# 128 bytes of unused SBUF ahead of the low parts of the input

## The reference, cut to what matters

```python
def _trunk(x, ...):
    for layer in range(DEPTH):                      # DEPTH = 2
        if layer % 2 == 0:
            m = _ab_mixer(x, ...)                   # x @ w_in_ab, attention and retention heads, @ w_out_ab
        else:
            m = _ssd_mixer(x, ...)                  # x @ w_in_ssd, convolution, scan, gate, @ w_out_ssd
        x = _layer_norm(DN_ALPHA * x + m, ...)
        f = _conv_ffn(x, ...)                       # (silu(g) * u) @ w_down, with g, u = conv(x @ w_up)
        x = _layer_norm(DN_ALPHA * x + f, ...)
```

## Time and profile before

| | |
|---|---|
| median of 3 runs | 3045.04 us (3043.46 to 3046.95) |
| the profiled execution, span | 3044.3 us |
| PE busy | 3001.3 us (99%) |
| PEld busy (beside PE) | 2936.1 us (96%) |
| DVE busy | 1977.1 us (65%) |
| ACT busy | 1623.5 us (53%) |
| matmuls of L664 to L666 | 3 x 7552 = 22,656 |
| mean granted TensorE clock | 0.995 |

### The profile page before, as it was taken

One profiled execution on the slowest core, in us unless ns is written; L12 is line 12 of the kernel. 1 busy time (PEld: TensorE's weight loads), 2 busy tenths in 40 slices (PEclk: granted clock), 3 DMA queues, 4 the chain that ended last, 5 costly groups with the idle time before them and its releaser, 6 DMA issues.

```text
span 3044.3 us, 60261 instructions
## 1 busy us (share of the span) xinstructions
PE 3001.3 (99%) x25064; PEld 2936.1 (96%) x25064; DVE 1977.1 (65%) x2508; ACT 1623.5 (53%) x1735; POOL 175.6 (6%) x317
## 2 busy tenths in 40 slices
PE   9999999999999999999999999999999999999997
PEld 9999899999999999999999999999999999999997
DVE  5454454677665566767767888876776665566665
ACT  4435575545444444545556767775564444445453
POOL 1010101000000000000002222210000000000000
PEclk9999999999999999999999999999999999999998
DMA  7565667544444545544467788874444444555452
GB/s 271 185 236 208 222 221 276 197 160 165 176 168 182 200 167 206 186 182 162 159 224 258 273 295 277 298 263 188 184 158 185 188 165 179 193 194 177 181 191 83
DMA packets 100667, 614.99 MB, mean 202 GB/s; under 512 B 12912, under 2 KB 13184, under 8 KB 39456
## 3 DMA queue, kind: packets, MB, share of 16 engines
q1 hardware_dynamic: 68688, 498.17, 43.8%
q0 software_dynamic: 31824, 114.61, 11.3%
HBM read 575.44 MB, written 37.28 MB: 201 GB/s over the span
## 4 chain that ended last, share of the span: by engine, by line
PE 90%; DVE 5%; ACT 2%; issue 1%; DMA 1%; POOL 0%; DVEq 0%; POOLq 0%; SPq 0%; ACTq 0%
PE acc L664 29%; PE acc L665 28%; PE acc L666 28%; DVE lo L574 1%; PE aux L2130 1%; DMA extra<-xds 1%; DVE x L1816 1%; DVE xl L1829 1%; DVE x L1824 1%; PE aux L2479 0%; ACT hi L564 0%; PE aux L2460 0%; ACT xh L1223 0%; PE aux L2215 0%; PE aux L2228 0%
## 5 line engine op out<-in xcount | busy, mean ns | idle before, releaser
L664 PE MATMUL acc<-xh,hi 128*128 128x264 f32 x7552 | 2177.3, 288 | 9.2 <-DVE lo L574 4.2
L665 PE MATMUL acc<-xl,hi 128*128 128x264 f32 x7552 | 2147.3, 284 | 0.0
L666 PE MATMUL acc<-xh,lo 128*128 128x264 f32 x7552 | 2139.6, 283 | 0.0
L664 PEld LDWEIGHTS acc<-xh,hi 128*128 128x128 f32 x7552 | 1423.6, 189 | 31.1 <-issue 19.5
L665 PEld LDWEIGHTS acc<-xl,hi 128*128 128x128 f32 x7552 | 1423.6, 189 | 1.8
L666 PEld LDWEIGHTS acc<-xh,lo 128*128 128x128 f32 x7552 | 1420.5, 188 | 0.0
L574 DVE TENSOR_TENSOR lo<-raw,hi 128x2048 fp32r<-128x2048 f32 x473 | 1077.5, 2287 | 378.8 <-ACT hi L564 378.0
L564 ACT ACTIVATE hi<-raw 128x2048 fp32r<-128x2048 f32 x473 | 897.7, 1907 | 490.0 <-DMA raw<-in_w 322.4
L563 ACT ACTIVATE xh<-pj 128x1056 fp32r<-128x1056 f32 x144 | 156.0, 1084 | 338.2 <-PE acc L666 279.8
L571 DVE TENSOR_TENSOR xl<-pj,xh 128x1056 fp32r<-128x1056 f32 x144 | 180.7, 1255 | 201.8 <-ACT hi L564 199.3
L1539 DVE SCALAR_TENSOR_TENSOR stage<-acc,par,stage 128x255 f32<-128x255 f32 x352 | 168.7, 479 | 23.1 <-DVE stage L1539 21.9
(11 more groups left out here) (287 smaller groups left out, 1617.3 us busy)
## 6 DMA issues: line engine op xcount, KB each, us to landing
raw<-in_w SPq DMA_DIRECT2D x473, 1024.0 KB, 4.9
x<-in_ssm POOLq DMA_DIRECT2D x32, 512.0 KB, 7.4
out_ssms<-x POOLq DMA_DIRECT2D x32, 512.0 KB, 7.2
x<-in_ret POOLq DMA_DIRECT2D x16, 512.0 KB, 5.6
out_rets<-x POOLq DMA_DIRECT2D x16, 512.0 KB, 4.3
x<-in_ck POOLq DMA_DIRECT2D x16, 512.0 KB, 4.4
x<-in_cv POOLq DMA_DIRECT2D x16, 512.0 KB, 5.8
pj<-cumd POOLq DMA_DIRECT2D x32, 256.0 KB, 7.2
```

Of the source, the lines that this page charges most:

```text
L664: pe.matmul(out, hi[:, s, w], xh[:, a, :], start=kc == 0 and k == 0, stop=False)
L665: pe.matmul(out, hi[:, s, w], xl[:, a, :], start=False, stop=False)
L666: m = pe.matmul(out, lo[:, r, w], xh[:, a, :], start=False, stop=kc == ph.kc - 1 and k == CK - 1)
```

## The change

One line is added: a buffer of 32 floats (128 bytes of each partition) between `xh` and `xl`, which nothing reads or writes. `raw`, `lo`, `x` and `xh` keep their places; `xl`, `pj`, `hi` and everything behind begin 128 bytes later. No instruction, semaphore or transfer is added, removed or put in another order.

```diff
         x_ = sb("x", [P, KT * T])
         xh = sb("xh", [P, KT, T], F32R)
+        sb("row_half", [P, 32])
         xl = sb("xl", [P, KT, T], F32R)
         pj = sb("pj", [P, AB_TILES * T])
```

## The result

The changed kernel takes 3057.22 us (median), against 3046.84 us for the kernel before beside it. The ratio is 1.0039, with a 95% interval of 1.0029 to 1.0049: slower by some 12 us (the medians are 10.4 us apart), where no change was forecast. The profiled execution has a span of 3057.7 us against 3044.3, 13.4 us more.

The account below looks back on a forecast made before the run. PE's step from product to product was taken to bound the kernel. Swapped chunk times added 0.4 us, all else 0: 3044.7 us on the span, 3045.4 us as median; likeliest 3045 us, 8-in-10 range 3029 to 3064 us.

Parts of the forecast that it names:

- What bounds the kernel: Whole kernel: PE, busy 99% of the span, sets the time by its step between products (L664 to L666); no producer does.
- That 128 bytes count, and as a distance modulo 256: Products in up0: even chunks take 5.80 us, odd ones 5.85, because input tiles start 128 bytes apart modulo 256.
- Which operands meet: L664 to L666: passing tile meets weights loaded for the next product: `xh` with `hi`, `xl` with `lo`, `xh` with next `hi`.
- term 1: Products: all three tile-weight pairs shift by 128 bytes, so even and odd chunks swap 5.80 and 5.85 us; +0.4 us.
- The bounds from the nearest steps: Products: every step of twelve like the fastest, 1.44 us, or the slowest, 1.47 us; 3014 to 3071 us.
- rival A: Loads of `hi` in L664 and L665: the weights' own place costs 16 us, giving 3061 us; 0.22 together with the mirror of B.
- the mirror of B: Products: the passing tile's own place puts all even chunks at 5.85 us, 12 us slower, 3057 us; 0.22 together with rival A.
- The mean over all places: Input tiles: each of eight 32-byte steps modulo 256 occurs twice in 16 tiles, so the trace already holds the mean.
- rival B: Products: the tile's own place costs only when `xh` and `xl` share it; 12 us faster, 3033 us; 0.20 with anything quicker.
- a longer pair of chunks: Sign in up0's timeline: a pair longer by 0.07 us means rival A, one at 11.70 us the mirror of B.
- Rival C: Buffer placement: `xl` and `hi` end at the same places modulo 256, so steps stay and time is 3045 us; chance 0.05.
- Terms 2 to 4: DVE and ACT lines, transfers, and the 2408 smaller matmuls of PE: each taken as 0.

Follow-up runs that it names:

- e3_xh_xl: Kernel before with `xh` and `xl` moved by 128 bytes, `lo` and `hi` keeping their places modulo 256: 3046.33 us, ratio 1.0001.
- p2_probe: Kernel before with measuring products put ahead: places of `xl` and `hi` scanned, then two tiles alternating with two weight blocks; pairs of chunks took 11.62 to 11.77 us.
- e1_xl_only: Kernel before with only `xl` moved by 128 bytes, what lies behind it put back: 3043.13 us, ratio 0.9992.
- f1_strided: Kernel before with a chunk's four input tiles four places apart in `xh` and `xl`, whose starts were also shifted: 3047.95 us, ratio 1.0004.

## Why the prediction was wrong

- **What bounds the kernel** was right. PE sets the time, at nothing that it waits for, and no other engine's pace changed. The signal that was to warn of a producer, L664's idle time, stayed at 9 us.
- **That 128 bytes count, and as a distance modulo 256** was right: 256 bytes give the times of before, all four buffers moved give the times of none moved, and with PE alone running the steps are the same. The rows that showed it, even and odd chunks, were the right ones to read.
- **Which operands meet** is the step that failed. From the starts of the loads the prediction took three pairs, each tile with the weights that are loaded while it passes, and concluded that moving `xl` and `hi` shifts all of them alike. `e3_xh_xl` shifts exactly these three and gives the swap that was forecast, 5.85 and 5.80; the change gives 5.86 and 5.85. What differs between the two is the distance of a tile to the weights of its own product (`xl` to `hi` in L665, `xh` to `lo` in L666), and `p2_probe` shows that with the prediction's pairs held fixed this difference moves the step as well, by 2.4 ns a product at 128 bytes. Of the four distances between tiles and weights the change shifts two (`xh` to `hi`, `xl` to `lo`) and leaves two, so an even chunk doesn't become an odd one, but something that the trace of before doesn't hold.
- **The size** of term 1 was put at +0.4 us and measured at 0.06 x 236 = 14 us. The bounds from the nearest steps, 3014 to 3071 us, held it. So did the range of 3029 to 3064, but by luck: its upper part was there for rival A and the mirror of B, and the reasons of both fall.
- **The mean over all places** was the reason for standing near the middle, and it doesn't carry: the step is no sum over distances, as the table of four shows, and with the same distances it takes one of two values by what ran before. The kernel before lay near the better end of what such shifts can give, so a shift was more likely to lose than to leave the time alone.
- **Rival A** named 3061 us, near the result, for a reason that falls: `hi` moved alone costs nothing. Its count of runs was the wrong way round besides, since the blocks of `hi` lay 128 past a multiple of 256 before the change and on one after it. **The mirror of B** named what was seen, even chunks at 5.85, a pair of 11.70 and 3057 us, and its reason falls as well: in `e1_xl_only` the tiles lie as in the changed kernel, and a pair takes 11.63 us. By the same two runs **rival B**'s own place of the tile falls, though `xl` alone does bring a pair down by 0.02 us. So a longer pair of chunks, which was to be the sign of A or of the mirror, had a cause that was neither. **Rival C** falls: the steps changed.
- **Terms 2 to 4** held: DVE and ACT are within 1 ns of the earlier trace rows, and the chunks account for the whole difference.
- **The two rules of the Trainium skill.** By the independent ports that the Trainium skill gives in "SBUF — State Buffer", "Who interferes with whom", the distance of the two reads would cost nothing, and that doesn't hold here: with DVE, ACT, POOL and the transfers idle, places of tiles and weights against each other made 0.06 us in a pair of chunks, or 120.0 against 126.9 ns at fixed places. The step of 112.5 ns, the estimate for a lone matmul from the Trainium skill's "TensorE: Matmul & The Clock Gate", "Back-to-back issue gap", was reached nowhere: the smallest step seen with 264 columns is 116.7 ns.

What stays open is how the two reads hold each other up. The runs show a period of 256 bytes, an effect of more than the prediction's three pairs and of what ran ahead; no run shows what the two reads share. Why the corner of the table costs 0.06 us and its neighbours nothing was not derived.

## What to carry to other kernels

Where one engine is busy throughout, read the distance between its starts by address, not only by shape: here steps that repeated closely and differed between equal instructions were a matter of place. Such an effect isn't to be added up buffer by buffer: here neither of two moves cost anything, and both together did. Some thousand products ahead of the kernel measured sixteen layouts in one run and agreed with the whole kernels, but a layout whose step depends on what ran ahead must be tried in place. The order of the products within an accumulation counts beside the places: together they were worth 20 us here, while the best move of `xl` and `hi` alone in the scan brought a pair from 11.65 to 11.62 us.

## What the runs showed of the hardware

- The step of PE depended on the places of passing tiles and weights against each other, modulo 256 bytes: with 264 columns of float32r and 128 columns of weights it was between 116.7 and 126.9 ns, with nothing else running.
- The same places gave 120.3 or 121.7 ns by what ran ahead, with PE alone; and 120.0 ns with PE alone but 123.3 ns in the whole kernel `f1_strided`.
- At 128 columns of tile the step stopped at 111 ns with 128 columns of weights and fell to 60 ns with 64, and weights of 32 columns in place of 128 didn't shorten the step of 264 columns (121 ns).
